# The entry of x: squares per token tile, the norm factor in a diagonal matrix, parameter loads and S5 columns moved

## The chip, the cores and the metric

The kernel runs on one core of one Trainium2 chip. Each engine (TensorE, VectorE, ScalarE, GpSimd, SyncE) works through its own queue of instructions; semaphores order them against each other. The metric is the device time of one execution in microseconds.

## The reference

One layer of a hybrid model on x of 512 tokens by 2048 (fp32). What matters here is its entry:

```python
def rms_norm(x, g):
    xf = x.astype(jnp.float32)
    y = xf * lax.rsqrt(jnp.mean(xf * xf, axis=-1, keepdims=True) + NORM_EPS)
    return (y * g.astype(jnp.float32)).astype(x.dtype)
# h = rms_norm(x, norm_mix); the columns of h @ w_in feed four mixers:
# s5_mixer, rglru_mixer, rwkv7_mixer, ssd_mixer
```

The four mixers' outputs (512 columns each) are joined and multiplied by w_out, x is added, a second norm follows, then a mixture of 64 experts of which each token uses two, and a last norm. The S5 mixer needs small tables made from its parameters (lambda, log_dt, B, C): exponentials, cosines and sines of phases, and B scaled by them.

## The kernel before

**How the work is staged.** A token tile is 128 tokens (NTT = 4 tiles), P = 128. Nearly everything lives in one large buffer `big`; the trace shows all its parts by that name. The stages are: entry of x (load, norm, turn so that the 2048 model columns lie on the partitions: `hT`, 16 k-blocks of 128 by 512 tokens), 38 projection tiles h @ w_in (L2096, each 16 k-blocks of 128x512, weights through two slabs that take turns, `ring`), with the mixers' work between the tiles, then the RWKV mixer, the output projection, routing and the experts (L2416, L2430, L2445), and the final norm (L1092 to L1094). There is no planner for the part that the change touches: the order on each engine's queue is the order of the code of its block.

**The entry, by engine.**

- SyncE (L479 to L505) issues the loads of x, one per token tile, waits for GpSimd's clearing of the parameter tables (`zero_ok`), issues the 22 loads of the tables A and B and two of mu (L491 to L494; each row of a table is 128 parameters), and then slab 0 and slab 1 of w_in (L502). From slab 2 on a slab waits for the tiles that used the slab two before it.
- ScalarE (L796 to L833) issues the loads of the S5 parameters (L797 to L804), waits for each tile of x and squares it with a running sum (L808), issues further small loads (cbc, lora, lru: L812 to L820), takes one square root for all four tiles (L822), and then the exponentials and sines for S5. After that it copies each projection tile out of PSUM (L849, `proj_out`).
- VectorE (L1102 to L1134) waits for all four sums, computes mean plus eps and its reciprocal (L1103, L1105), scales the four tiles of x in place once the root is there (L1108), copies the turned parameter tables out of PSUM (colA, colB, colC: L1111 to L1119), and multiplies the turned x by norm_mix while it copies it from PSUM into `hT` (L1132, 16 banks of 128x512). Then come the S5 phases (L1147 to L1183) and B scaled (L1216).
- TensorE (L1904 to L1921) transposes the tables A and B and the S5 columns (L1906, L1907, L1910), then x in 64 blocks of 128x128, four to a PSUM bank, with four banks taking turns (L1919), waits until all 16 banks are read (L1921), and starts the projection tiles. Behind tile 3 it turns the S5 matrices (`s5_setup`, L1929, L1935), and from tile 4 on every 11th projection matmul is followed by one S5 step (L1946, L1955).
- GpSimd (L622 to L701) clears buffers, makes the identity (`const_ok`, L640) and masks, copies the scaled B into block-diagonal form (L679), and makes the tables of cosines and sines of the 16 S5 pairs (L693 to L701), two ahead.

Of the kernel before, what the change touches and what calls it, by code (L numbers as in the profile page):

```python
# [99 lines left out]
MS, LDT, S5COL, SPA, LRDT, PHASE1, PHASE2, BBAR, SP_ = range(1, 10)  # L100
# [3 lines left out]
def build(nc, I, out):  # L104
    with ExitStack() as ctx:
# [23 lines left out]
        wk = big[:, 70:78, :]  # L129
        wglu = big[:, 78:82, :]  # L130
# [263 lines left out]
        prm_in = sem("prm_in")  # L394
# [3 lines left out]
        wglu_in, lruw_in, lora_in = sem("wglu_in"), sem("lruw_in"), sem("lora_in")  # L398
# [5 lines left out]
        h_ok = sem("h_ok")  # L404
# [68 lines left out]

        block = ctx.enter_context(nc.Block())

        @block.sync
        def _(sp):
# [3 lines left out]
            for s, (c0, wd) in enumerate(slabs):  # L481
                if s == 0:

                    sp.wait_ge(zero_ok, 1)
                    for tab, dst in ((PA, prmA), (PB, prmB)):
                        for name, (r, n) in tab.items():
                            src = I[name]
                            flat = src.rearrange(" ".join("abcd"[:len(src.shape)]) + " -> (" + " ".join("abcd"[:len(src.shape)]) + ")")
                            if name == "rw_mu":
                                flat = flat[0:3 * W]  # L490
                            sp.dma_start(dst[r:r + n, :], flat.rearrange("(r c) -> r c", c=P)).then_inc(prm_in, 16)  # L491
                    mu = I["rw_mu"]
                    sp.dma_start(prmB[MU_LORA:MU_LORA + 1, 0:LW + LA], mu[:, 3 * W:3 * W + LW + LA]).then_inc(prm_in, 16)
                    sp.dma_start(prmB[MU_LORA + 1:MU_LORA + 2, 0:LG], mu[:, 3 * W + LW + LA:]).then_inc(prm_in, 16)  # L494
# [125 lines left out]
        def _(pool):  # L620
# [5 lines left out]
            nc.gpsimd.memset(misc[:, :], 0.0)  # L626
            nc.gpsimd.memset(prmA, 0.0)
            nc.gpsimd.memset(prmB, 0.0).then_inc(zero_ok, 1)
            nc.gpsimd.memset(lruW, 0.0).then_inc(zero_ok, 1)
            nc.gpsimd.memset(epsb[:], EPS)  # L630
# [163 lines left out]
        def _(act):  # L794
            a = Steps(act, act_s)
            act.wait_ge(zero_ok, 1)  # L796
            act.dma_start(ldt[:], I["s5_log_dt"][0].rearrange("(g u) -> g u", u=2)).then_inc(ldt_in, 16)  # L797
# [7 lines left out]

            for i in range(NTT):
                act.wait_ge(x_io[i], 16)
                nc.scalar.activation(hT[:, 0:4, :].rearrange("p a n -> p (a n)"), xs[:, i, :], ACT.Square,  # L808
                                     accum_out=st[:, i:i + 1]).then_inc(ssq_ok, 1)
                act.wait_ge(ssq_ok, i + 1)  # L810
            for k, w in enumerate(("ssd_dt_bias", "ssd_a_log", "ssd_d")):
                act.dma_start(cbc[:, k, :], I[w].to_broadcast([P, SH])).then_inc(cbc_in, 16)  # L812
            act.dma_start(loraW[0:LW, 0, :], I["rw_w2"][0]).then_inc(lora_in, 16)
            act.dma_start(loraW[LW:LW + LA, 0, :], I["rw_a2"][0]).then_inc(lora_in, 16)
            act.dma_start(loraW[0:LG, 1, :], I["rw_g2"][0]).then_inc(lora_in, 16)
            act.wait_ge(zero_ok, 2)
            for r, w in enumerate(("lru_wa", "lru_wx")):
                wv = I[w][0].rearrange("(t u) i j -> u i t j", u=2)
                for u in range(2):
                    act.dma_start(lruW[64 * u:64 * u + 64, r, :, 64 * u:64 * u + 64], wv[u]).then_inc(lruw_in, 16)  # L820
            act.wait_ge(setup_ok, MS)
            nc.scalar.activation(st[:, 8:12], st[:, 4:8], ACT.Sqrt).then_inc(rs_ok, 1)  # L822
# [4 lines left out]
            nc.scalar.activation(s5v[:, 2, :], s5v[:, 1, :], ACT.Exp).then_inc(mag_ok, 1)  # L827
            act.wait_ge(setup_ok, PHASE2)
# [16 lines left out]

            def proj_out(n):
                s, c, wd, d = tiles[n]
                act.wait_ge(proj_ok, n + 1)
                nc.scalar.activation(proj[0:wd, d, :], ps[n % 2][0:wd, :], ACT.Copy).then_inc(proj_got, 1)  # L849
# [65 lines left out]
            for n in range(NT):  # L915
                if n == NT - 1:
                    take("rms_s", zroot, ACT.Sqrt, bias=epsb[:], scale=1.0 / W)
                proj_out(n)
# [177 lines left out]
        NPRM = 16 * (len(PA) + len(PB) + 2)  # L1096

        @block.vector
        def _(dve):
            v = Steps(dve, dve_s)  # L1100

            dve.wait_ge(ssq_ok, NTT)  # L1102
            v.do(nc.vector.tensor_scalar(st[:, 12:16], st[:, 0:4], 1.0 / D, EPS, ALU.mult, ALU.add))  # L1103
            v.settle()
            v.tell(nc.vector.reciprocal(st[:, 4:8], st[:, 12:16]), setup_ok, MS)  # L1105
            dve.wait_ge(rs_ok, 1)
            for i in range(NTT):
                v.tell(nc.vector.tensor_scalar(xs[:, i, :], xs[:, i, :], st[:, 8 + i:9 + i], None, ALU.mult), h_ok, i + 1)  # L1108

            dve.wait_ge(prm_tr, 1)  # L1110
            nc.vector.tensor_copy(colA[:], ps[6][:, 0:128])  # L1111
            nc.vector.tensor_copy(colB[:], ps[6][:, 128:256]).then_inc(prm_col, 1)
            dve.wait_ge(prm_col, 1)

# [3 lines left out]
            dve.wait_ge(prm_tr, 2)  # L1118
            v.tell(nc.vector.tensor_copy(colC[:], ps[7][:, 0:48]), setup_ok, S5COL)  # L1119
# [7 lines left out]

            for m in range(NTT * 4):
                i, c4 = divmod(m, 4)
                dve.wait_ge(tr_ok, m + 1)  # L1130
                g0 = PB["norm_mix"][0] + 4 * c4
                nc.vector.tensor_tensor(  # L1132
                    hT[:, 4 * c4:4 * c4 + 4, P * i:P * (i + 1)], ps[2 + m % 4][:].rearrange("p (a n) -> p a n", a=4),
                    colB[:, g0:g0 + 4].to_broadcast([P, 4, P]), ALU.mult).then_inc(tr_used, 1)  # L1134
# [768 lines left out]
        def _(pe):  # L1903
# [580 lines left out]
```

## Time and profile before

| | |
|---|---|
| median of 3 runs | 2699.86 us (2698.58 to 2702.86) |
| profiled execution, its own time | 2699.62 us |
| its span | 2697.8 us |
| TensorE matmul busy | 2366.5 us (88%) |
| VectorE, ScalarE, GpSimd busy | 760.6, 351.6, 372.2 us |
| chain that ended last | TensorE 49%, DMA 38%, VectorE 8% |

The times of the rows below are microseconds from the span's start. The chain of waits is followed back from the last instruction, at each step to what released it; "ACTq" and "SPq" are the instruction queues of ScalarE and SyncE (issues of DMAs), PEld is TensorE's weight load. An fp32 matmul that is not a transposition appears as two weight loads and two matmuls.

### The profile page before, as it was taken

Reading aid. Unit: us, or ns where it says so; the run is one execution under the profiler, and the core shown is the slowest. Engines: PE = TensorE matmul, PEld = TensorE weight load, DVE = VectorE, ACT = ScalarE, POOL = GpSimd, SP = SyncE. Lnnn points to the kernel's source line nnn. Section 1 sums busy time; section 2 is a strip of 40 time slices with the busy share of each in tenths; the row PEclk is TensorE's granted clock in tenths of the full one; section 3 lists DMA queues with packets and bytes.
Section 4 is the critical chain, followed back from the end, with each engine's and each line's share of the span. In section 5 each row is a group of like instructions: output and inputs, shape, how many; then the busy total and the mean of one; then the engine's idle time right before and its main releaser. Section 6 shows DMA issues by size and latency. Waiting matters only on the chain.

```text
span 2697.8 us, 31798 instructions
## 1 busy us (share of the span) xinstructions
PE 2366.5 (88%) x12861; PEld 1277.0 (47%) x12861; DVE 760.6 (28%) x1158; ACT 351.6 (13%) x641; POOL 372.2 (14%) x501
## 2 busy tenths in 40 slices
PE   3999999999989999869888888888888888888883
PEld 2443344455467876534444444444444444444441
DVE  4298925423553433421111000011110100111114
ACT  2100013110322222200000000000000000000001
POOL 2265500000012210011111111111011111110110
PEclk9999999999989999979999999999999999899996
DMA  5221111112022124489999999999999999999986
GB/s 147 63 78 31 63 62 52 63 63 85 4 87 72 48 72 165 175 349 428 429 429 429 426 426 418 418 421 420 413 428 415 420 415 416 419 406 410 424 376 272
DMA packets 127328, 724.00 MB, mean 268 GB/s; under 512 B 33848, under 2 KB 93052, under 8 KB 98332
## 3 DMA queue, kind: packets, MB, share of 16 engines
q1 hardware_dynamic: 100188, 704.75, 63.7%
q0 software_dynamic: 18720, 16.84, 1.8%
q10 hardware_dynamic: 8352, 1.44, 0.4%
q8 instruction: 51, 0.84, 0.1%
q14 instruction: 17, 0.14, 0.0%
HBM read 724.39 MB, written 49.81 MB: 287 GB/s over the span
## 4 chain that ended last, share of the span: by engine, by line
PE 49%; DMA 38%; DVE 8%; issue 2%; ACT 1%; ACTq 1%; SPq 1%; POOL 0%; POOLq 0%; DVEq 0%
DMA big<-in_moe_w 37%; PE ps L2096 16%; PE ps L2416 15%; PE ps L2148 5%; DVE big L1137 3%; PE ps L2314 2%; PE ps L2445 1%; PE ps L2229 1%; PE ps L2214 1%; DVE big L1267 1%; DVE big L1266 1%; PE ps L1955 1%; PE ps L1977 1%; PE ps L2335 0%; DMA big<-h_rows,gix 0%
## 5 line engine op out<-in xcount | busy, mean ns | idle before, releaser
L2416 PE MATMUL ps<-big 128*64 128x384 f32 x4096 | 715.7, 510 | 126.7 <-DMA big<-in_moe_w 126.4
L2416 PEld LDWEIGHTS ps<-big 128*64 128x64 f32 x4096 | 350.7, 143 | 503.6 <-issue 345.5
L2096 PE MATMUL ps<-big 128*128 128x512 f32 (+2 forms) x1216 | 533.1, 597 | 3.4 <-DVE big L1132 1.7
L2445 PE MATMUL ps<-big 128*64 128x512 f32 x1536 | 381.0, 650 | 51.7 <-DVE big L1870 51.7
L2096 PEld LDWEIGHTS ps<-big 128*128 128x128 f32 (+2 forms) x1216 | 227.6, 189 | 299.9 <-issue 295.8
L1867 DVE COPY big<-ps 128x384 f32<-128x384 f32 x64 | 35.7, 558 | 796.5 <-PE ps L2416 796.5
L2445 PEld LDWEIGHTS ps<-big 128*64 128x64 f32 x1536 | 113.4, 147 | 271.8 <-issue 211.2
L2148 PE MATMUL ps<-big 128*128 128x256 f32 x768 | 186.0, 391 | 12.4 <-ACT big L889 8.3
L774 POOL COPY six<-idxs 128x1 int32 (+1 forms) x64 | 11.6, 181 | 1203.1 <-DVE big L1874 1203.1
L2148 PEld LDWEIGHTS ps<-big 128*128 128x128 f32 x768 | 141.8, 191 | 38.6 <-issue 13.4
L1874 DVE COPY big<-ps 128x512 f32<-128x512 f32 x64 | 44.3, 692 | 390.4 <-PE ps L2445 390.4
L2430 PE MATMUL ps<-stacked,big 128*128 128x64 f32 x768 | 140.9, 333 | 0.0
L2430 PEld LDWEIGHTS ps<-stacked,big 128*128 128x128 f32 x768 | 138.8, 261 | 0.0
L1075 ACT ACTIVATE big<-ps 128x384 f32<-128x384 f32 x64 | 31.4, 491 | 803.7 <-PE ps L2416 803.7
L1137 DVE TENSOR_TENSOR big<-big 128x512 f32<-128x512 f32 (+8 forms) x136 | 112.3, 847 | 46.5 <-ACT big L854 41.2
L1081 ACT ACTIVATE big<-ps 128x512 f32<-128x512 f32 x64 | 38.2, 597 | 414.8 <-PE ps L2445 414.8
L849 ACT ACTIVATE big<-ps 128x512 f32<-128x512 f32 (+2 forms) x38 | 22.6, 595 | 504.2 <-PE ps L2096 504.2
L2402 PE MATMUL ps<-ident,big 128*128 128x128 f32 x520 | 71.9, 282 | 13.5 <-DMA big<-h_rows,gix 13.5
L2402 PEld LDWEIGHTS ps<-ident,big 128*128 128x128 f32 x520 | 56.4, 142 | 52.0 <-issue 52.0
L767 POOL DMA_INDIRECT big<-h_rows,gix x66 | 69.0, 1046 | 58.9 <-POOL gix L764 55.9
L777 POOL DMA_INDIRECT y_rows<-big,six x64 | 65.2, 1019 | 59.2 <-POOL six L774 55.7
L724 POOL MEMSET big<- 64x512 f32 x8 | 4.0, 517 | 453.9 <-DVE big L1557 437.5
(387 smaller groups left out, 1734.0 us busy)
## 6 DMA issues: line engine op xcount, KB each, us to landing
big<-in_moe_w SPq DMA_DIRECT2D x192, 3072.0 KB, 32.1
big<-in_w_in SPq DMA_DIRECT2D x18, 2048.0 KB, 8.6
big<-in_w_out SPq DMA_DIRECT2D x8, 1024.0 KB, 5.9
big<-y_rows SPq DMA_DIRECT2D x8, 1024.0 KB, 11.8
big<-in_x SPq DMA_DIRECT2D x4, 1024.0 KB, 8.6
big<-in_w_out SPq DMA_DIRECT2D x8, 512.0 KB, 7.0
big<-in_x SPq DMA_DIRECT2D x16, 256.0 KB, 2.7
big<-in_w_out SPq DMA_DIRECT2D x1, 4096.0 KB, 14.7
```

What stands on the lines that cost most here:

```text
L767: nc.gpsimd.indirect_dma_start(xg[k], None, hdg, bass.IndirectOffsetOnAxis(ap=gix[k][:, 0:1], axis=0), bounds_check=T * GR - 1, oob_is_err ...
L777: nc.gpsimd.indirect_dma_start(ydg, bass.IndirectOffsetOnAxis(ap=six[k][:, 0:1], axis=0), yb[k], None, bounds_check=2 * T * GR - 1, oob_is ...
L1081: nc.scalar.activation(yb[k][:, 0:512], ps[5][:], ACT.Copy).then_inc(y_ok[k], 1)
L1137: v.do(nc.vector.tensor_tensor(out, a, b, o))
L1874: nc.vector.tensor_copy(yb[k][:, 512 * q:512 * q + 512], ps[5 + q][:]).then_inc(y_ok[k], 1)
L2096: last = nc.tensor.matmul(ps[n % 2][0:wd, :], ring[s % 2][:, k, c:c + wd], hT[:, k, :], start=(k == 0), stop=(k == NC - 1))
L2148: last = nc.tensor.matmul(ps[b][:, 256 * i:256 * i + 256], ready[c][:, P * (2 * h + i):P * (2 * h + i) + P], w, start=(j == 0), stop=(j == ...
L2314: last = nc.tensor.matmul(o[:], V_[:, q, P * i:P * i + P], wo_rw[:, q, 512 * ncol:512 * ncol + 512], start=(q == 0), stop=(q == WT - 1))
L2402: last = nc.tensor.transpose(ps[h][:, P * j:P * j + P], xg[k][:, P * c:P * c + P], ident[:])
L2416: last = nc.tensor.matmul(ps[2 + w][B * g:B * g + B, 0:FF], xT[k][:, j, B * g:B * g + B], W13[k][w][:, NJ * g + j, :], start=(j == 0), sto ...
L2430: last = nc.tensor.matmul(o, uv[k][:, w, :].rearrange("p (t c) -> p c t", c=FC)[:, m], stacked[:], start=True, stop=True)
L2445: last = nc.tensor.matmul(ps[5 + q][B * g:B * g + B, :], hid[k][:, m, :], W2[k][:, m, 512 * n:512 * n + 512], start=(m == 0), stop=(m == F ...
```

## The change

Each token tile of x is squared as soon as it has landed, and its root is taken at once. VectorE puts the reciprocal of the root on the diagonal of a 128x128 matrix (`rdiag`), and x is turned by an ordinary product with this matrix in the place of the transposition; x is not scaled any more. The loads of table B (with norm_mix) and of mu go from SyncE to ScalarE's queue, ahead of the squares; those of table A go behind slab 0 on SyncE's queue; the S5 loads go behind the roots on ScalarE's queue. The turning of table A and of the S5 columns stands behind projection tile 0, VectorE's copies of them behind the banks of x, and ScalarE's copy of tile 0 ahead of its wait for the phases. The projection's first tile waits for the banks of the last token tile one by one. The rest are renamed semaphores.

```diff
--- before.py
+++ after.py
@@ -97,7 +97,7 @@
-MS, LDT, S5COL, SPA, LRDT, PHASE1, PHASE2, BBAR, SP_ = range(1, 10)
+MS, LDT, S5COL, SPA, LRDT, PHASE1, PHASE2, BBAR, SP_ = range(4, 13)
 MU_LORA = 72
@@ -127,6 +127,7 @@
         wk = big[:, 70:78, :]
+        rdiag = big[:, 76, :]
         wglu = big[:, 78:82, :]
@@ -391,17 +392,16 @@
         x_io = [sem(f"x_io{i}") for i in range(NTT)]
-        prm_in = sem("prm_in")
+        prm_in, prmB_in = sem("prm_in"), sem("prmB_in")
         s5_in = sem("s5_in")
...
         wdt_in = sem("wdt_in")
-        wglu_in, lruw_in, lora_in = sem("wglu_in"), sem("lruw_in"), sem("lora_in")
+        wglu_in, gates_in = sem("wglu_in"), sem("gates_in")
         dve_s, act_s, pool_s = sem("dve_step"), sem("act_step"), sem("pool_step")
...
         setup_ok, rs_ok = sem("setup_ok"), sem("rs_ok")
-        h_ok = sem("h_ok")
         tr_ok, tr_used = sem("tr_ok"), sem("tr_used")
@@ -471,6 +471,14 @@
+        def params(eng, tab, dst, done):
+            for name, (r, n) in tab.items():
+                src = I[name]
+                flat = src.rearrange(" ".join("abcd"[:len(src.shape)]) + " -> (" + " ".join("abcd"[:len(src.shape)]) + ")")
+                if name == "rw_mu":
+                    flat = flat[0:3 * W]
+                eng.dma_start(dst[r:r + n, :], flat.rearrange("(r c) -> r c", c=P)).then_inc(done, 16)
@@ -479,19 +487,9 @@
             for s, (c0, wd) in enumerate(slabs):
-                if s == 0:
...
+                if s == 1:
                     sp.wait_ge(zero_ok, 1)
-                    for tab, dst in ((PA, prmA), (PB, prmB)):
-                        for name, (r, n) in tab.items():
-                            src = I[name]
-                            flat = src.rearrange(" ".join("abcd"[:len(src.shape)]) + " -> (" + " ".join("abcd"[:len(src.shape)]) + ")")
-                            if name == "rw_mu":
-                                flat = flat[0:3 * W]
-                            sp.dma_start(dst[r:r + n, :], flat.rearrange("(r c) -> r c", c=P)).then_inc(prm_in, 16)
-                    mu = I["rw_mu"]
-                    sp.dma_start(prmB[MU_LORA:MU_LORA + 1, 0:LW + LA], mu[:, 3 * W:3 * W + LW + LA]).then_inc(prm_in, 16)
-                    sp.dma_start(prmB[MU_LORA + 1:MU_LORA + 2, 0:LG], mu[:, 3 * W + LW + LA:]).then_inc(prm_in, 16)
+                    params(sp, PA, prmA, prm_in)
                 if s == 5:
@@ -624,10 +622,10 @@
             nc.gpsimd.memset(misc[:, :], 0.0)
+            nc.gpsimd.memset(epsb[:], EPS)
             nc.gpsimd.memset(prmA, 0.0)
...
             nc.gpsimd.memset(lruW, 0.0).then_inc(zero_ok, 1)
-            nc.gpsimd.memset(epsb[:], EPS)
             nc.gpsimd.memset(eps64[:], 64e-5)
@@ -794,6 +792,19 @@
             act.wait_ge(zero_ok, 1)
+            params(act, PB, prmB, prmB_in)
+            mu = I["rw_mu"]
+            act.dma_start(prmB[MU_LORA:MU_LORA + 1, 0:LW + LA], mu[:, 3 * W:3 * W + LW + LA]).then_inc(prmB_in, 16)
+            act.dma_start(prmB[MU_LORA + 1:MU_LORA + 2, 0:LG], mu[:, 3 * W + LW + LA:]).then_inc(prmB_in, 16)
+            nc.scalar.activation(st[:, 40:41], epsb[:], ACT.Sqrt)
...
+            for i in range(NTT):
+                act.wait_ge(x_io[i], 16)
+                if i:
+                    act.wait_ge(ssq_ok, i)
+                nc.scalar.activation(wide(88), xs[:, i, :], ACT.Square, accum_out=st[:, i:i + 1]).then_inc(ssq_ok, 1)
+                act.wait_ge(ssq_ok, i + 1)
+                nc.scalar.activation(st[:, 4 + i:5 + i], st[:, i:i + 1], ACT.Sqrt, bias=epsb[:], scale=1.0 / D).then_inc(rs_ok, 1)
             act.dma_start(ldt[:], I["s5_log_dt"][0].rearrange("(g u) -> g u", u=2)).then_inc(ldt_in, 16)
@@ -802,29 +813,27 @@
-            for i in range(NTT):
-                act.wait_ge(x_io[i], 16)
-                nc.scalar.activation(hT[:, 0:4, :].rearrange("p a n -> p (a n)"), xs[:, i, :], ACT.Square,
-                                     accum_out=st[:, i:i + 1]).then_inc(ssq_ok, 1)
-                act.wait_ge(ssq_ok, i + 1)
             for k, w in enumerate(("ssd_dt_bias", "ssd_a_log", "ssd_d")):
                 act.dma_start(cbc[:, k, :], I[w].to_broadcast([P, SH])).then_inc(cbc_in, 16)
-            act.dma_start(loraW[0:LW, 0, :], I["rw_w2"][0]).then_inc(lora_in, 16)
-            act.dma_start(loraW[LW:LW + LA, 0, :], I["rw_a2"][0]).then_inc(lora_in, 16)
-            act.dma_start(loraW[0:LG, 1, :], I["rw_g2"][0]).then_inc(lora_in, 16)
+            act.dma_start(loraW[0:LW, 0, :], I["rw_w2"][0]).then_inc(gates_in, 16)
+            act.dma_start(loraW[LW:LW + LA, 0, :], I["rw_a2"][0]).then_inc(gates_in, 16)
+            act.dma_start(loraW[0:LG, 1, :], I["rw_g2"][0]).then_inc(gates_in, 16)
             act.wait_ge(zero_ok, 2)
...
                 for u in range(2):
-                    act.dma_start(lruW[64 * u:64 * u + 64, r, :, 64 * u:64 * u + 64], wv[u]).then_inc(lruw_in, 16)
-            act.wait_ge(setup_ok, MS)
-            nc.scalar.activation(st[:, 8:12], st[:, 4:8], ACT.Sqrt).then_inc(rs_ok, 1)
+                    act.dma_start(lruW[64 * u:64 * u + 64, r, :, 64 * u:64 * u + 64], wv[u]).then_inc(gates_in, 16)
...
+            def proj_out(n):
+                s, c, wd, d = tiles[n]
+                act.wait_ge(proj_ok, n + 1)
+                nc.scalar.activation(proj[0:wd, d, :], ps[n % 2][0:wd, :], ACT.Copy).then_inc(proj_got, 1)
...
             nc.scalar.activation(s5v[:, 2, :], s5v[:, 1, :], ACT.Exp).then_inc(mag_ok, 1)
+            proj_out(0)
             act.wait_ge(setup_ok, PHASE2)
@@ -842,11 +851,6 @@
-            def proj_out(n):
-                s, c, wd, d = tiles[n]
-                act.wait_ge(proj_ok, n + 1)
-                nc.scalar.activation(proj[0:wd, d, :], ps[n % 2][0:wd, :], ACT.Copy).then_inc(proj_got, 1)
@@ -915,7 +919,8 @@
                     take("rms_s", zroot, ACT.Sqrt, bias=epsb[:], scale=1.0 / W)
-                proj_out(n)
+                if n:
+                    proj_out(n)
                 if n == 3:
@@ -1093,45 +1098,47 @@
-        NPRM = 16 * (len(PA) + len(PB) + 2)
...
-            dve.wait_ge(ssq_ok, NTT)
-            v.do(nc.vector.tensor_scalar(st[:, 12:16], st[:, 0:4], 1.0 / D, EPS, ALU.mult, ALU.add))
-            v.settle()
-            v.tell(nc.vector.reciprocal(st[:, 4:8], st[:, 12:16]), setup_ok, MS)
-            dve.wait_ge(rs_ok, 1)
-            for i in range(NTT):
-                v.tell(nc.vector.tensor_scalar(xs[:, i, :], xs[:, i, :], st[:, 8 + i:9 + i], None, ALU.mult), h_ok, i + 1)
...
+            dve.wait_ge(const_ok, 1)
...
+            def rms_diag(i):
+                dve.wait_ge(rs_ok, i + 1)
+                v.do(nc.vector.reciprocal(st[:, 8 + i:9 + i], st[:, 4 + i:5 + i]))
+                v.settle()
+                v.tell(nc.vector.tensor_scalar(rdiag[:, P * i:P * i + P], ident[:], st[:, 8 + i:9 + i], None, ALU.mult), setup_ok, i + 1)
...
+            rms_diag(0)
             dve.wait_ge(prm_tr, 1)
-            nc.vector.tensor_copy(colA[:], ps[6][:, 0:128])
             nc.vector.tensor_copy(colB[:], ps[6][:, 128:256]).then_inc(prm_col, 1)
...
-            dve.wait_ge(ldt_in, 16)
-            v.tell(nc.vector.tensor_copy(prmC[0:16, :].rearrange("p (u n) -> p u n", u=2),
-                                         ldt[:].unsqueeze(2).to_broadcast([NPAIR, 2, S5_N])), setup_ok, LDT)
-            dve.wait_ge(prm_tr, 2)
-            v.tell(nc.vector.tensor_copy(colC[:], ps[7][:, 0:48]), setup_ok, S5COL)
-            v.settle()
-            lr, li = colC[:, 16:32], colC[:, 32:48]
...
-            ap4 = colA[:, PA["lru_a_param"][0]:PA["lru_a_param"][0] + WT]
-            v.do(nc.vector.tensor_scalar(lsp[:, 2, :], ap4, -1.0, None, ALU.mult))
-            v.settle()
-            v.tell(nc.vector.tensor_tensor(lsp[:, 0, :], ap4, lsp[:, 2, :], ALU.max), setup_ok, SPA)
...
                 i, c4 = divmod(m, 4)
+                if c4 == 2 and i + 1 < NTT:
+                    rms_diag(i + 1)
                 dve.wait_ge(tr_ok, m + 1)
...
                     colB[:, g0:g0 + 4].to_broadcast([P, 4, P]), ALU.mult).then_inc(tr_used, 1)
+            dve.wait_ge(ldt_in, 16)
+            v.tell(nc.vector.tensor_copy(prmC[0:16, :].rearrange("p (u n) -> p u n", u=2),
+                                         ldt[:].unsqueeze(2).to_broadcast([NPAIR, 2, S5_N])), setup_ok, LDT)
+            dve.wait_ge(prm_tr, 2)
+            nc.vector.tensor_copy(colA[:], ps[6][:, 0:128]).then_inc(prm_col, 1)
+            dve.wait_ge(prm_col, 2)
+            dve.wait_ge(prm_tr, 3)
+            v.tell(nc.vector.tensor_copy(colC[:], ps[7][:, 0:48]), setup_ok, S5COL)
+            v.settle()
+            lr, li = colC[:, 16:32], colC[:, 32:48]
...
+            ap4 = colA[:, PA["lru_a_param"][0]:PA["lru_a_param"][0] + WT]
+            v.do(nc.vector.tensor_scalar(lsp[:, 2, :], ap4, -1.0, None, ALU.mult))
+            v.settle()
+            v.tell(nc.vector.tensor_tensor(lsp[:, 0, :], ap4, lsp[:, 2, :], ALU.max), setup_ok, SPA)
@@ -1902,23 +1909,25 @@
             pe.wait_ge(const_ok, 1)
-            pe.wait_ge(prm_in, NPRM)
-            nc.tensor.transpose(ps[6][:, 0:128], prmA, ident[:])
+            pe.wait_ge(prmB_in, 16 * (len(PB) + 2))
             nc.tensor.transpose(ps[6][:, 128:256], prmB, ident[:]).then_inc(prm_tr, 1)
-            pe.wait_ge(setup_ok, LDT)
-            pe.wait_ge(s5_in, 16 * 8)
-            nc.tensor.transpose(ps[7][:, 0:48], prmC, ident[0:48, 0:48]).then_inc(prm_tr, 1)
             for m in range(NTT * 4):
...
                 if c4 == 0:
-                    pe.wait_ge(h_ok, i + 1)
+                    pe.wait_ge(setup_ok, i + 1)
                 if m >= 4:
...
                     c = 4 * c4 + j
-                    last = nc.tensor.transpose(ps[2 + m % 4][:, P * j:P * (j + 1)], xs[:, i, P * c:P * (c + 1)], ident[:])
+                    last = nc.tensor.matmul(ps[2 + m % 4][:, P * j:P * (j + 1)], xs[:, i, P * c:P * (c + 1)], rdiag[:, P * i:P * i + P],
+                                            start=True, stop=True)
                 last.then_inc(tr_ok, 1)
-            pe.wait_ge(tr_used, NTT * 4)
+            def s5_params():
+                pe.wait_ge(prm_in, 16 * len(PA))
+                nc.tensor.transpose(ps[6][:, 0:128], prmA, ident[:]).then_inc(prm_tr, 1)
+                pe.wait_ge(setup_ok, LDT)
+                pe.wait_ge(s5_in, 16 * 8)
+                nc.tensor.transpose(ps[7][:, 0:48], prmC, ident[0:48, 0:48]).then_inc(prm_tr, 1)
@@ -1986,7 +1995,7 @@
                 pe.wait_ge(conv_ok, WT)
-                pe.wait_ge(lruw_in, 64)
+                pe.wait_ge(gates_in, 48 + 64)
                 for q in range(WT):
@@ -2093,6 +2102,8 @@
                 for k in range(NC):
+                    if n == 0 and k % 4 == 0:
+                        pe.wait_ge(tr_used, NTT * 4 - 3 + k // 4)
                     last = nc.tensor.matmul(ps[n % 2][0:wd, :], ring[s % 2][:, k, c:c + wd], hT[:, k, :],
@@ -2101,6 +2112,8 @@
                 last.then_inc(proj_ok, 1)
+                if n == 0:
+                    s5_params()
                 if n == 3:
@@ -2152,7 +2165,7 @@
             pe.wait_ge(lot_ok, 2)
-            pe.wait_ge(lora_in, 48)
+            pe.wait_ge(gates_in, 48 + 64)
             for q in range(WT):
```

## Rows read from the trace of the kernel before

**Rows 1.** Chain of waits, 0 to 200 us: start us, us, what.

```profile
3.62 8.17 ACTq L801
...
21.30 2.01 ACT big L808 x2
...
34.97 1.28 ACT L822
...
48.52 6.08 DVE big L1132 x10
54.64 56.91 PE ps L2096 x128
...
138.44 1.89 DVE big L1137 x3
```

**Rows 2.** Timeline, 0 to 60 us: start us, us, engine, line, what [idle before].

```profile
1.58 0.44 ACTq L797 DMA_DIRECT2D ldt<-in_s_log_dt  x1
...
7.35 0.29 POOL L640 TENSOR_SCALAR_AFFINE_SELECT ident<-ident 128x128 f32<-128x128 f32 x1 [0.16 <-POOL big L638]
...
11.71 6.64 SPq L502 DMA_DIRECT2D big<-in_w_in  x2
...
36.50 4.87 DVE L1108 TENSOR_SCALAR big<-big,st 128x2048 f32<-128x2048 f32 x4 [6.68 <-ACT st L822]
41.29 0.28 DVE L1111 COPY colA<-ps 128x128 f32<-128x128 f32 x1
...
42.08 0.34 PE L1910 MATMUL ps<-ident,big 48*128 48x48 f32 x1 [23.12 <-DVE big L1116]
```

**Rows 3.** Two source lines, L479 and L804: issues, then their landing times.

```profile
L479 SPq DMA_DIRECT2D big<-in_x x4: 393/426/659, 0.8 to 2.2; - x4
...
DMA to landing us min/median/max: 4.9/8.6/12.3
...
L804 ACTq DMA_DIRECT2D big<-in_s_c_im x2: 976/1362/1748, 17.2 to 18.2; - x2
DMA to landing us min/median/max: 7.2/10.1/11.8
```

**Rows 4.** DMA issues, 0 to 60 us: KB each, median us to landing.

```profile
big<-in_w_in SPq DMA_DIRECT2D x2, 2048.0 KB, 17.3
...
big<-in_s_lambda_im ACTq DMA_DIRECT2D x1, 8.0 KB, 5.7
```

**Rows 5.** Timeline of ScalarE, 2673 to 2677 us, in the final norm.

```profile
2674.01 1.91 ACT L1092 ACTIVATE big<-big 128x2048 f32<-128x2048 f32 x1 [1.28 <-DVE big L1893]
...
2676.05 0.29 ACT L1094 ACTIVATE st<-st,epsb 128x1 f32<-128x1 f32 x1
```

**Rows 6.** Timeline of TensorE's matmuls, 560 to 565 us.

```profile
563.05 0.39 PE L2040 MATMUL ps<-maskneg,ident 128*128 128x128 f32 x2
563.27 0.39 PE L2038 MATMUL ps<-tri,sds 128*128 128x128 f32 x2
```

**Rows 7.** Stretches: length; busy us (count) of PE, PEld, DVE, ACT, POOL; clock, DMA, GB/s.

```profile
3.00:13.00 10.00, 0.00 (x0) 0.00 (x0) 0.00 (x0) 0.00 (x0) 9.30 (x22) 1.00 1.00 399
...
42.30:48.50 6.20, 6.20 (x31) 6.16 (x31) 4.69 (x9) 0.22 (x1) 0.00 (x0) 1.00 0.00 0
48.50:52.80 4.30, 4.30 (x36) 3.60 (x34) 4.29 (x8) 0.00 (x0) 0.00 (x0) 1.00 0.00 0
...
54.60:58.60 4.00, 3.96 (x6) 1.66 (x7) 3.69 (x12) 1.50 (x2) 0.00 (x0) 0.57 0.02 4
```

**Rows 8.** Timeline, 60 to 145 us.

```profile
64.25 0.84 ACT L829 ACTIVATE big<-big 128x768 f32<-128x768 f32 x1 [7.95 <-DVE big L1183]
...
70.38 0.60 ACT L849 ACTIVATE big<-ps 128x512 f32<-128x512 f32 x1 [3.03 <-PE ps L2096]
...
84.11 0.60 ACT L849 ACTIVATE big<-ps 128x512 f32<-128x512 f32 x1 [13.14 <-PE ps L2096]
...
87.14 1.26 POOL L701 TENSOR_TENSOR big<-big 128x512 f32<-128x512 f32 x1
```

More of the change, by code:

```diff
@@ L1100, in _ @@
             v = Steps(dve, dve_s)
-            dve.wait_ge(ssq_ok, NTT)
-            v.do(nc.vector.tensor_scalar(st[:, 12:16], st[:, 0:4], 1.0 / D, EPS, ALU.mult, ALU.add))
-            v.settle()
-            v.tell(nc.vector.reciprocal(st[:, 4:8], st[:, 12:16]), setup_ok, MS)
-            dve.wait_ge(rs_ok, 1)
-            for i in range(NTT):
-                v.tell(nc.vector.tensor_scalar(xs[:, i, :], xs[:, i, :], st[:, 8 + i:9 + i], None, ALU.mult), h_ok, i + 1)
+            dve.wait_ge(const_ok, 1)
[5 more added lines that the diff above has]
+            rms_diag(0)
             dve.wait_ge(prm_tr, 1)
-            nc.vector.tensor_copy(colA[:], ps[6][:, 0:128])
             nc.vector.tensor_copy(colB[:], ps[6][:, 128:256]).then_inc(prm_col, 1)
             dve.wait_ge(prm_col, 1)
+            for m in range(NTT * 4):
+                i, c4 = divmod(m, 4)
+                if c4 == 2 and i + 1 < NTT:
+                    rms_diag(i + 1)
+                dve.wait_ge(tr_ok, m + 1)
+                g0 = PB["norm_mix"][0] + 4 * c4
+                nc.vector.tensor_tensor(
+                    hT[:, 4 * c4:4 * c4 + 4, P * i:P * (i + 1)], ps[2 + m % 4][:].rearrange("p (a n) -> p a n", a=4),
+                    colB[:, g0:g0 + 4].to_broadcast([P, 4, P]), ALU.mult).then_inc(tr_used, 1)
             dve.wait_ge(ldt_in, 16)
@@ L1126, in _ @@
             v.tell(nc.vector.tensor_tensor(lsp[:, 0, :], ap4, lsp[:, 2, :], ALU.max), setup_ok, SPA)
[L1128 to L1134, printed above, removed]
             def op(out, a, b, o):
```

## The prediction

> **What bounds the kernel now.** I read the chain of waits first, because the change touches only the first 55 us and the question is which engine holds the start there. Up to 54.64 us no projection runs. The chain lies on ScalarE's queue: the issue of one small load alone takes 8.17 us, the first square waits behind it until 21.3, the square root comes at 34.97 (a table load, then the root) and the first projection starts at 54.64 [rows 1]. The timeline adds what lies between the last two: VectorE scales x for 4.9 us, and TensorE turns it from 42.3 on, after 23 us of idleness [rows 2]. ScalarE had no reason in x for being so late: the four x loads are issued from 0.8 us on, the first is there 4.9 us after its issue, the last 12.3 us after its own [rows 3]. From 54.64 on the chain is TensorE's projection tiles, and from about 138.4 on VectorE's S5 pairs [rows 1], which TensorE's steps between the tiles feed. Nothing in these rows is tied to an absolute time, so what the start gains or loses should reach the end one to one.
>
> I measure the change at one landmark: the end of projection tile 1, where ScalarE begins to copy it at 84.11 us [rows 8]. By then the moved S5 columns have been paid as well.
>
> **ScalarE's new order.** It issues 6 DMAs (4 of table B, 2 of mu) from 1.6 us on, such an issue takes 0.44 us [rows 2], so they are out at about 4.3. Table load 1.28 [rows 1], one small Sqrt 0.29 [rows 5]: 5.9. Tile 0 of x has landed at 0.8 + 4.9 = 5.7. In the final norm Square and Sqrt of one tile take from 2674.01 to 2676.05 plus 0.29 = 2.33 us, and no table load stands between the roots and squares there [rows 5], so the alternation costs none here. Root of tile 0: about 8.3. Tile 3 lands at 2.2 + 12.3 = 14.5 [rows 3]; its root is there at 16.9. This replaces the common root after 34.97 + 1.28. The S5 issues that stalled ScalarE now come behind the roots.
>
> **VectorE.** Out: the two small operations on the sums and the four scalings of x, 4.87 us on the path [rows 2]. In: per tile one reciprocal and one 128x128 product with a column scalar. The trace has no such product; a 128x128 copy out of PSUM takes 0.28 [rows 2]. With the small reciprocal and two hand-overs, 0.4 to 0.8; I take 0.55. Diagonal 0 is there at 8.9, the last at 17.5.
>
> **Table B.** Its last issue is at about 4.3. A like small load on ScalarE's queue under the same x traffic landed 5.7 us after its issue [rows 4]: 10.0. The lower bound is no delay at all, 4.3 (the start would then wait for diagonal 0, 8.9), the upper one the landing of x itself, 14.5. I take 10.0. One transposition more: 10.5. The identity, complete at 7.6 [rows 2], is no limit. So TensorE starts to turn x at 10.5 rather than 42.3.
>
> **The turning product.** This is the part that gets dearer. Now it is 64 transpositions of one pass; afterwards 64 ordinary fp32 products with 128 columns, of two weight loads and two matmuls each. The trace has just these in another stage: the two instructions of one line there take 0.22 us (563.05 to 563.27) [rows 6], so 0.223 us a block at full clock, 0.446 at half. Before, the transpositions ran 31 in 6.2 us and then 36 in 4.3 us [rows 7]. The clock column gives 1.00 for both; it is the rate that tells that TensorE came out of its idleness at the lower of its two levels (1.2 GHz) and rose to 2.4 GHz at 48.5. I take the same 6.2 us for the new start: 13.9 blocks at 0.446, then 50.1 at 0.223 = 11.2 us, together 17.4. VectorE's drains, 6.08 us for 10 banks [rows 1], so 2.4 for four, plus the diagonal make 3.0 us a token tile against TensorE's 16 x 0.223 = 3.6, so TensorE paces it; tile 3's diagonal comes long before its turn at 24. The first projection starts at 10.5 + 17.4 = 27.9. It needn't wait for the last banks, since k-blocks 0 to 3 need bank 13 only.
>
> The Trainium skill, page Perfetto Trace Analysis, section Transposes, says that a logical transposition should be a transpose and not a standard matmul. The trace agrees on the price: 0.223 a block instead of 0.12 at full clock. By this rule alone the change would lose 64 x 0.103 = 6.6 us; what the rule leaves out is that the product lets the scalings and the wait for all four tiles go.
>
> **Slab 0 of w_in.** Now issued at 11.71 behind the parameters [rows 2], afterwards at about 2.9 directly behind x. Before, the two slabs landed 17.3 us after their issue in the middle, together with the S5 loads [rows 4]. Afterwards x is through at about 13, and at 399 GB/s [rows 7] 2.1 MB more take 5.3: it lands at about 20. The upper bound is the old landing, 11.7 + 17.3 = 29.0, one us behind 27.9. I take no cost.
>
> **Tiles 0 and 1, and the S5 columns between them.** Tile 0 took 70.38 - 54.64 = 15.74 us [rows 1, 8]. In its first four us the granted clock was 0.57 in the mean, so half of full for most of them [rows 7], right after transpositions paced by VectorE; that cost 4.0 x 0.43 = 1.7. With TensorE now in ordinary products without a gap I let the clock hold: 14.0. Then come the two transpositions, 0.34 us for the small one [rows 2] and about as much for the other, 0.6 in all. Tile 1: 13.7 (70.38 to 84.11). Landmark: 27.9 + 14.0 + 0.6 + 13.7 = 56.2 against 84.1, 27.9 us earlier.
>
> **What the moved steps wait for.** The two transpositions behind tile 0 wait for the S5 loads, and tile 1, next in TensorE's queue, with them. These loads are now issued from 17 us on. Before, the last of them, c_im, was issued at 18.2 and took up to 11.8 to land: 30.0, some 17 us after x was through [rows 3]. Afterwards 17 + 12 to 17 + 17, so 29 to 34, while tile 0 ends at 41.9. The slack of 8 us is the cover; without it each microsecond of lateness is one at the end. Table A rides behind slab 0 on SP's queue, slab 1 behind it; it is needed at 56.
>
> The Trainium skill, page DMA: Bandwidth & Descriptors, section Queues, rings and completion order, says that each DMA engine goes round robin between the queues, a packet at a time. This fits the 8.17 us issue: ScalarE's small packets advance one by one beside x's. By it the S5 loads get through faster beside slab 1's short rows than beside x, the lower end of 29 to 34.
>
> VectorE copies the S5 columns (colC) at about 42.4, as before, so relative to the projections 28 us later. What hangs on them took 64.25 - 54.6 = 9.7 us to the phases (the sines begin there), and 24.2 more to GpSimd's second table, complete at 88.4 [rows 8]. Afterwards: 52.1 and 76.3. TensorE's S5 set-up stands behind tile 3, at 56.2 + 2 x 13.7 = 83.6, and GpSimd's block copies that it needs come before the tables. No cost, slack over 7 us. ScalarE's copy of tile 0 now stands before its wait for the phases, so tile 2 isn't held.
>
> **Sum.** 2699.62 (the profiled execution's own time; span 2697.8 and 1.8 around it) - 27.9 = 2671.7. That execution lies 0.24 below the median of the three runs, 2699.86; I forecast 2672.
>
> **Rivals.**
> 1. *TensorE stays at the lower clock through the turning* (chance 0.12). For it: the rows of this form cover only some products in a stage that was fast before. Against it: even transpositions saw the clock rise after 6.2 us [rows 7]. Turning 64 x 0.446 = 28.5, projection from 39.0, tile 0 again 1.7 dearer: 12.8 us less gained, 2684.6.
> 2. *The start hangs on a load* (0.10): table B or x's tile 3 comes later, or slab 0 at 31 rather than 20, because an issue is held up by a full queue as the 8.17 us one was [rows 1]. 3 to 6 us less gained: 2675 to 2678.
> 3. *The S5 loads hold tile 1 back* (slower; 0.03). The place is TensorE's wait behind tile 0. It costs one to one what they come after 41.9, and turns the whole into a loss from 41.9 + 27.9 = 69.8 on; at 80 us it would be 2710. For it: the longest issue of the whole start is one of these. Against it: before, they were through at 30.0 though begun beside x.
> 4. *The gain is taken back later* (0.02, no change, 2700): the S5 pairs or the expert stage turn out paced by something that does not start earlier. No row of the chain shows such a thing.
>
> **From this to the numbers.** Forecast 0.73, at 2672. Its own spread: TensorE's start at 8.9 and half the time at the lower clock give 2669; table B at 14 and a lower clock once more in tile 0 give 2677.5; stretches of lower clock in later stages may come or go, some 2 us either way. The range 2667 to 2682 takes in rival 2 and leaves out rivals 1, 3 and 4. A difference of 0.2%, 5.4 us, is what a measurement here can tell from none. Faster by more: 0.73 + 0.12 + 0.10 = 0.95; within: 0.02; slower: 0.03.
>
> **What would show it.** ScalarE: four pairs of square and root between 6 and 17 us, no table load among them. TensorE: first product at 10 to 11, 128 matmuls over 17 to 18 us with the rate doubling inside them, first projection at 27 to 29, at full clock from its first matmul, slab 0 landed before. Between tiles 0 and 1 less than 1 us without a projection. The VectorE piece at 138.44 comes at about 110.5, and each later stage 28 us earlier. The forecast is wrong if a block keeps taking 0.43 us, if TensorE waits for a load at about 42, or if that VectorE piece comes less than 25 us earlier.

## The result and the profile after

The changed kernel takes 2672.59 us (median of 4 runs, 2669.5 to 2673.07) against 2701.36 before: ratio 0.9893, 95% interval 0.988 to 0.9906. Forecast 2672. Run again beside its variants (r1_change) it gave 2671.77 against 2700.11, ratio 0.9903 (0.9886 to 0.9919). The profiled execution took 2669.5, the lowest of the four, with a span of 2667.7. The intervals of both ratios lie below 1, so the gain of about 1% is clear of the scatter.

The chain of waits of the changed kernel, 0 to 200 us (start us, us, what):

```profile
2.09 0.67 ACTq L480
...
4.25 5.83 DMA big<-in_rw_mu
10.66 16.65 PE ps L1922 x128
27.31 13.73 PE ps L2107 x32
41.34 41.41 PE ps L2107 x96
...
109.64 1.89 DVE big L1144 x3
```

Of ScalarE's queue only the short issues of table B's loads are left in it, until 4.25; the stalled issues of the S5 loads are gone. The last load of table B (the second one of mu) holds TensorE until 10.1, then the chain is TensorE's to 82.8. VectorE's piece that stood at 138.44 [rows 1] stands at 109.64, 28.8 earlier.

One long issue is left at the start, in another queue. SyncE's first small load behind slab 0 took 9.68 us to issue, and 10.78 in e4_s5_first; the same load directly behind x, with no slab ahead of it, took 0.41 before and 0.52 in e1_order.

```profile
3.63 9.68 SPq L480 DMA_DIRECT2D big<-in_s_d  x1
```

Here nothing waits for it, since table A is first used at 40.9. Why such an issue takes so long, no run shows; that the queue was full, as rival 2 of the prediction has it, is a guess.

The timeline of the changed kernel (start us, us, engine, line, what, [idle before <- releaser]) answers to rows 2 and 5:

```profile
4.59 1.28 ACT L799 ACT_TABLE_LOAD   x1 [4.59 <-issue]
5.89 0.20 ACT L799 ACTIVATE st<-epsb 128x1 f32<-128x1 f32 x1
6.13 1.91 ACT L805 ACTIVATE big<-big 128x2048 f32<-128x2048 f32 x1
...
8.56 0.17 DVE L1110 RECIPROCAL st<-st 128x1 f32<-128x1 f32 x1 [8.56 <-ACT st L807]
8.76 0.36 DVE L1112 TENSOR_SCALAR big<-ident,st 128x128 f32<-128x128 f32 x1
...
10.21 0.45 PE L1913 MATMUL ps<-ident,big 128*128 128x128 f32 x1 [10.21 <-DMA big<-in_rw_mu]
...
13.75 1.91 ACT L805 ACTIVATE big<-big 128x2048 f32<-128x2048 f32 x1 [0.17 <-DMA big<-in_x]
...
15.79 0.29 ACT L807 ACTIVATE st<-st,epsb 128x1 f32<-128x1 f32 x1
...
27.15 13.90 PE L2107 MATMUL ps<-big 128*128 128x512 f32 x32
...
55.31 0.60 ACT L830 ACTIVATE big<-ps 128x512 f32<-128x512 f32 x1 [0.42 <-PE ps L2107]
```

The last row is the landmark, the copy of tile 1: 55.31 instead of 84.11 [rows 8], 28.8 earlier, forecast 27.9. The stretches of the changed kernel (columns as in rows 7) show the rate of the product and the clock of tile 0:

```profile
10.40:15.70 5.30, 5.30 (x27) 5.30 (x27) 2.03 (x5) 5.07 (x8) 4.41 (x14) 1.00 1.04 376
15.70:27.10 11.40, 11.40 (x104) 11.40 (x104) 9.47 (x17) 0.35 (x2) 2.61 (x4) 1.00 1.14 282
27.10:31.10 4.00, 4.00 (x12) 1.85 (x12) 0.85 (x3) 0.00 (x0) 0.00 (x0) 1.00 0.95 181
```

27 matmuls in 5.3 us are 0.196 each, 104 in 11.4 are 0.110: half speed first, then full, as the transpositions had it before [rows 7]. The two stretches together count 131 for the 128, since table B's transposition falls into the first and what spans a border is counted on both sides. The column of the granted clock gives 1.00 for both, as it did for the transpositions; the lower level is read off the rate alone. Tile 0 runs at 1.00, without the 0.57 of before.

### The profile page after: what moved, and what is told of

It is laid out like the page before. It is cut to its first block, busy times and chain, and to the rows that moved or that the text cites. A ratio compares the mean times of both kernels' runs of the same rounds, so it can differ in the third digit from the quotient of the medians.

```text
span 2667.7 us, 31933 instructions
## 1 busy us (share of the span) xinstructions
PE 2368.4 (89%) x12925; PEld 1283.9 (48%) x12925; DVE 758.4 (28%) x1160; ACT 351.7 (13%) x644; POOL 372.7 (14%) x501
## 4 chain that ended last, share of the span: by engine, by line
PE 50%; DMA 38%; DVE 8%; issue 2%; ACT 1%; SPq 1%; POOL 0%; ACTq 0%; POOLq 0%; DVEq 0%
DMA big<-in_moe_w 37%; PE ps L2107 17%; PE ps L2429 15%; PE ps L2161 5%; DVE big L1144 3%; PE ps L2327 2%; PE ps L2458 1%; PE ps L2242 1%; PE ps L2227 1%; DVE big L1274 1%; DVE big L1273 1%; PE ps L1922 1%; PE ps L1964 1%; PE ps L1986 1%; PE ps L2348 0%
## 5 line engine op out<-in xcount | busy, mean ns | idle before, releaser
L2429 PE MATMUL ps<-big 128*64 128x384 f32 x4096 | 729.5, 518 | 127.2 <-DMA big<-in_moe_w 126.7
L2458 PE MATMUL ps<-big 128*64 128x512 f32 x1536 | 365.7, 628 | 51.8 <-DVE big L1877 51.8
```

What stands on the lines that cost most here:

```text
L2429: last = nc.tensor.matmul(ps[2 + w][B * g:B * g + B, 0:FF], xT[k][:, j, B * g:B * g + B], W13[k][w][:, NJ * g + j, :], start=(j == 0), sto ...
L2458: last = nc.tensor.matmul(ps[5 + q][B * g:B * g + B, :], hid[k][:, m, :], W2[k][:, m, 512 * n:512 * n + 512], start=(m == 0), stop=(m == F ...
```

## The experiments

"Landmark" is the start of ScalarE's copy of projection tile 1 in the profiled execution; "rest" is that execution's span less its landmark.

| run | landmark | first projection | span | rest | time (median) |
|---|---|---|---|---|---|
| before | 84.11 | 54.64 | 2697.8 | 2613.7 | 2700 to 2701 |
| changed | 55.31 | 27.15 | 2667.7 | 2612.4 | 2672.59 |
| e1_order | 72.78 | 45.01 | 2689.7 | 2616.9 | 2691.93 |
| e2_order_columns | 61.40 | 33.24 | 2675.2 | 2613.8 | 2680.81 |
| e3_scale_turn | 54.07 | 24.88 | 2672.5 | 2618.4 | 2671.26 |
| e4_s5_first | 73.55 | 45.39 | 2691.9 | 2618.4 | 2692.14 |
| e5_tableB_sync | 59.98 | 31.81 | 2677.7 | 2617.7 | 2679.43, one run |
| e6_all_banks | 56.15 | 27.91 | 2672.3 | 2616.2 | 2674.05, one run |
| e7_columns_first | 76.28 | 48.50 | 2696.1 | 2619.8 | 2697.92, one run |
| e8_warm | 52.93 | 24.77 | 2667.9 | 2615.0 | 2669.69, one run |
| r1_change | 54.44 | 26.27 | 2670.7 | 2616.3 | 2671.77 |
| r2_scale_turn | 54.09 | 25.09 | 2672.8 | 2618.7 | 2671.30 |
| r3_warm | 52.99 | 24.82 | 2667.0 | 2614.0 | 2669.81 |
| r4_warm_tableB_late | 52.15 | 23.98 | 2665.4 | 2613.3 | 2669.99 |

The code blocks below are the edits, shortened; lines with # say in words where they stand.

In all fourteen profiles the last projection copy comes 632.9 to 634.8 us behind the landmark; the scatter arises behind it. The rest scatters from 2612.4 to 2619.8; the changed kernel alone gives 2612.4 and 2616.3. So the landmark tells a microsecond or less, the time 3 to 7 us from one execution to the next. Before has only one profile, and 11 of the 13 others have a longer rest than its 2613.7: whether the later stages give back a microsecond or two of the gain stays open. In every run but the changed kernel's first the median gains less in time than the profile gains at the landmark (e1_order 8.2 and 11.3, e2_order_columns 19.3 and 22.7).

**e1_order**

```diff
 # ScalarE, in the kernel before
+ squares of the four tiles; wait MS; one Sqrt
  S5 loads (ldt, lambda, b, c)
- squares of the four tiles
  cbc, lora, lru loads
- wait MS; one Sqrt
```

> The kernel before, with one change on ScalarE's queue: squares and the common root stand ahead of the S5 loads; scaling, transposition and the S5 columns ahead of x stay. Theory (the columns hold TensorE as soon as ScalarE doesn't): root at about 17.5, x scaled by 23, but TensorE waits for the S5 loads, now issued from 18 us on, until 33 to 35; first projection at about 46.5 instead of 54.6, so 8 us less, ratio 0.997. Rival (the late root was the whole cost): the turning starts at about 20 and the first projection at about 33, 21 us less, ratio 0.992.

Ratio to before 0.9965 (0.9953 to 0.9978), 8.2 us less; landmark 11.3 earlier. The root comes at 17.2 instead of 36.3, but TensorE's rows show who holds it now:

```profile
17.52 0.45 PE L1906 MATMUL ps<-ident,big 128*128 128x128 f32 x1 [17.52 <-DMA big<-in_rw_mu]
17.76 0.42 PE L1907 MATMUL ps<-ident,big 128*128 128x128 f32 x1
32.88 0.31 PE L1910 MATMUL ps<-ident,big 48*128 48x48 f32 x1 [14.70 <-DMA big<-in_s_c_im]
```

The S5 loads, now behind the squares, keep it until 32.9. The theory holds, the rival's 33 is excluded. The 3 us more at the landmark than expected are 1.5 in the first projection (45.0) and 1.7 of the lower clock, which tile 0 did not have here (in the columns of rows 7, where before has 0.57 at this place):

```profile
45.00:49.00 4.00, 3.99 (x10) 1.84 (x11) 3.69 (x12) 1.50 (x2) 0.00 (x0) 1.00 0.01 4
```

**e2_order_columns**

```diff
 # e1_order, and
 # TensorE
- transpose(prmC) ahead of x
+ if n == 0: wait LDT; wait s5_in; transpose(prmC)   # behind projection tile 0
 # VectorE: the copies LDT and colC with SPA go behind the 16 banks
 # ScalarE: proj_out(0) ahead of its wait for PHASE2
```

> As e1_order, and the turning of the S5 columns with VectorE's copies of them moved behind projection tile 0; one root for all tiles, scaling and transposition stay. Theory: tile 0 scaled at 19.3, turning from about 19.5, first projection at 32.5, the lower clock again in tile 0; copy of tile 1 at about 62 instead of 84.1, 22 us less, ratio 0.992. Order alone then carries three quarters of the gain of 28.8. Rival (the product with the diagonal is what carries it): less than 12 us.

Ratio 0.993 (0.9913 to 0.9946), 19.3 us less; landmark 22.7 earlier, 22 expected. Two moves, the order on ScalarE's queue and the S5 columns behind tile 0, carry 22.7 of the 28.8, with one common root, scaling and transposition as before. The agreement with 22 is in part luck: the first projection came at 33.2 and not 32.5, and 1.7 of the 22.7 is the lower clock in tile 0, which was expected and did not come. At the first projection they carry 21.4 of 27.5.

**e3_scale_turn and r2_scale_turn**

```diff
 # the changed kernel
- tensor_scalar(rdiag[:, P*i:P*i+P], ident[:], st[:, 8+i:9+i], None, mult)
+ tensor_scalar(xs[:, i, :], xs[:, i, :], st[:, 8+i:9+i], None, mult)
- matmul(ps[2+m%4][...], xs[:, i, P*c:P*c+P], rdiag[:, P*i:P*i+P])
+ transpose(ps[2+m%4][...], xs[:, i, P*c:P*c+P], ident[:])
```

> The changed kernel, with the product undone: VectorE scales each token tile in place (four times 1.28 us) and TensorE transposes it; all orders and the root per tile stay. Theory: VectorE becomes the pace, 16 x 0.69 + 4 x 1.5 us, first projection at about 27.5 as with the product, tile 0 then 1.7 us dearer by the lower clock: copy of tile 1 at about 57.5 against 55.3, 2 us more than the changed kernel. Rival (the product is worth the scaling that it saves): first projection at 31 or later, 4 us or more. Other rival (the product is dearer than it is worth, 64 x 0.1 us): 3 to 6 us faster than the changed kernel.

> Scaling in place and transposition again, beside the product on the same chip. Theory (the landmark carries to the end): 1.2 us less than the changed kernel, 2670 to 2672. Rival (the lower clock that transpositions bring costs later): 1 to 3 us more than the changed kernel.

Ratio to before 0.9887 (0.987 to 0.9903) and 0.9894 (0.9878 to 0.9911); beside the product on the same chip 2671.30 against 2671.77, no difference that can be told. At the landmark it is 1.2 and 0.4 us earlier than the product, where e3's theory had it 2 later. The first projection came at 24.9 and not 27.5, for three reasons. VectorE drains a bank in 0.61 and not 0.69 when the banks stand ready, 1.3 us over 16. Tile 0 was scaled at 8.59, before table B was there, so that only three scalings lie on the path. And the first projection started 1.1 us before the last bank was drained. Against them the first drain began at 11.5, a microsecond later than assumed. VectorE's and TensorE's rows of e3_scale_turn:

```profile
8.59 1.29 DVE L1112 TENSOR_SCALAR big<-big,st 128x2048 f32<-128x2048 f32 x1
...
13.10 1.41 DVE L1112 TENSOR_SCALAR big<-big,st 128x2048 f32<-128x2048 f32 x1
14.44 2.46 DVE L1124 TENSOR_TENSOR big<-ps,colB 128x512 f32<-128x512 f32 x4
```

```profile
18.35 1.97 PE L1922 MATMUL ps<-ident,big 128*128 128x128 f32 x16 [1.81 <-DVE big L1112]
22.41 2.68 PE L1922 MATMUL ps<-ident,big 128*128 128x128 f32 x16 [2.10 <-DVE big L1112]
24.88 14.92 PE L2106 MATMUL ps<-big 128*128 128x512 f32 x32
```

TensorE turns a token tile in 2.0 us instead of 3.6 and waits for VectorE; VectorE needs 3.8 with the scaling. The two ways are worth the same within a microsecond: what the product spares VectorE it costs TensorE. Up to the first projection the transposition is 2.3 us ahead (1.2 beside r1_change); tile 0 then takes 14.8 us (14.6) instead of 13.7 at the lower clock, which stands here from 23.5 to 26.9:

```profile
23.50:26.90 3.40, 3.40 (x12) 2.37 (x10) 2.58 (x6) 0.00 (x0) 0.00 (x0) 0.50 1.17 326
```

**e4_s5_first**

```diff
 # the changed kernel, ScalarE
+ S5 loads ahead of the squares, behind table B
```

> The changed kernel, with the S5 loads issued ahead of the squares on ScalarE's queue again. Theory (the queue's stalled issues were the cost): issues until about 23, root of tile 0 at 25.6, turning from 26.2, first projection at about 43.5: 16 us of the gain of 28.8 go. Rival (loads interfere little, tiles of x are awaited anyway): under 3 us.

Ratio to before 0.9965 (0.9951 to 0.9979). The landmark is 18.2 us later than the changed kernel's, 16 expected. The issues end at 24.2 and the first root comes at 27.7; the loads cost ScalarE the time of its queue, nothing else: TensorE starts to turn at 28.6, 18.2 later, and from there to the landmark it takes 44.9 us in both kernels. The root is 2 us later than expected, and so is the landmark. Neither of the two moves is worth more than some 11 us without the other: the order alone gives 11.3 (e1_order), all the rest without the order 10.6 (this run), all the rest without the columns 7.8 (e7_columns_first).

```profile
13.51 7.98 ACTq L806 DMA_DIRECT2D big<-in_s_c_re  x2
21.52 2.70 ACTq L806 DMA_DIRECT2D big<-in_s_c_im  x2
24.25 1.28 ACT L807 ACT_TABLE_LOAD   x1 [24.25 <-issue]
```

**e5_tableB_sync**

```diff
- ScalarE: params(act, PB, prmB, prmB_in); 2 loads of mu
+ SyncE, behind x and ahead of slab 0: wait zero_ok; params(sp, PB, prmB, prmB_in); 2 loads of mu
```

> The changed kernel, with the loads of table B and mu on SyncE's queue behind x and ahead of slab 0. Theory (a load behind x in the same queue lands with x): table B turned at 14 to 16 instead of 10.2, first projection at 31 to 33 instead of 27.15, copy of tile 1 at 59 to 61 instead of 55.3. Rival (table B is hidden by the tiles of x): no change, 55.3.

Landmark 59.98, 4.7 us later; table B is turned at 14.54 instead of 10.21. In the queue of x, behind its 4 MB, these small loads come 4.3 us later than on ScalarE's queue (one run).

**e6_all_banks**

```diff
- if n == 0 and k % 4 == 0: wait(tr_used, 13 + k // 4)
+ if n == 0 and k == 0:     wait(tr_used, 16)
```

> The changed kernel, the first projection waits for all 16 banks at once as before the change. Theory: first projection at 28.2 instead of 27.15, copy of tile 1 at 56.3. Rival (a gap in TensorE's work brings the lower clock in tile 0 back): another 1.7 us, 58.

Landmark 56.15: 0.8 later than in the first profile of the change, no more than two executions of one kernel differ by (r1_change). TensorE's wait for VectorE in it is 0.87 us, so that much is the edit's; tile 0 ran at full clock (1.00), so this gap did not bring the lower clock in this one run.

**e7_columns_first**

```diff
 # the changed kernel
+ TensorE: wait LDT; wait s5_in; transpose(prmC) ahead of the product, not behind tile 0
+ VectorE: LDT and colC ahead of the 16 banks (the diagonals get a semaphore of their own)
```

> The changed kernel, the S5 columns turned and copied ahead of x again (their loads stay behind the roots). Theory (then TensorE waits for the last S5 load): turning of x from about 32, first projection at about 49, copy of tile 1 at about 77 instead of 55.3. Rival (the loads are quick when x is through): turning from about 22, copy of tile 1 at about 67.

Landmark 76.28, 21.0 later; the theory holds. TensorE's row tells when the last S5 load is there, the wait that the change hides behind tile 0:

```profile
31.92 0.31 PE L1918 MATMUL ps<-ident,big 48*128 48x48 f32 x1 [21.56 <-DMA big<-in_s_c_im]
```

From this row to the first projection it takes 16.6 us with the product, and 12.1 in e1_order with x scaled beforehand and transposed. Where everything waits for the same load, the way with the product is 4.5 us dearer.

**e8_warm and r3_warm**

```diff
 # the changed kernel, TensorE
+ wait zero_ok
+ for i in range(20): matmul(ps[7][:, 0:P], ones[:], ones[:])
```

> The changed kernel, and TensorE, which idles until 10.2 us, multiplies a matrix of ones by itself 20 times from about 1.6 us on (work that nobody reads). Theory (the slow first third of the turning is the clock after idleness): the turning runs at 0.223 us a block from its first one on, 14.3 us in all, first projection at about 24.8 instead of 27.15, copy of tile 1 at 52.9 instead of 55.3. Rival (the first blocks are slow for another reason, such as the wait for VectorE): no change.

> The changed kernel with 20 unused products of ones ahead. Theory: 2.4 us less than the changed kernel, ratio to it 0.9991. Rival (the later stages swallow it): no difference.

Landmark 52.93 and 52.99 (52.9 expected): 2.4 us before the first profile of the change, 1.5 before r1_change, whose own slow part was shorter. Stretches of e8_warm: the unused work takes over the slow part, and the product runs at full speed from its first block.

```profile
1.60:5.40 3.80, 3.76 (x18) 3.76 (x19) 0.00 (x0) 0.82 (x1) 3.76 (x7) 1.00 0.94 302
5.40:8.20 2.80, 2.72 (x25) 2.53 (x23) 0.00 (x0) 2.76 (x5) 2.64 (x7) 1.00 1.03 426
10.20:24.80 14.60, 14.60 (x130) 14.53 (x131) 11.86 (x22) 5.44 (x9) 7.20 (x17) 1.00 1.07 309
```

18 matmuls in 3.8 us, 25 in 2.8, then 130 in 14.6. So the slow part belongs to whatever TensorE does first after idleness, not to the product or to waits for VectorE. That it is the clock is inferred from the rate, which is half; the column gives 1.00. The time, 2669.81 (ratio to before 0.9893, 0.9877 to 0.991) against r1's 2671.77, points the same way but is within the scatter.

**r4_warm_tableB_late**

```diff
 # r3_warm, TensorE
- wait prmB_in; transpose(prmB) ahead of x
+ if m == 1: wait prmB_in; transpose(prmB)   # behind the second bank of x
```

> As r3_warm, and TensorE turns table B behind the second bank of x instead of ahead of the first, so that the product starts with diagonal 0 at about 9.0 and not with table B at 10.2. Theory: first projection at 23.6, copy of tile 1 at 51.8 (changed kernel 55.3, e8_warm 52.9), 3.5 us less than the changed kernel. Rival (VectorE, which gets norm_mix later, becomes the pace): first projection at 24.5 to 25, no gain over r3_warm.

Landmark 52.15, 0.8 us before r3_warm; 1.1 were expected. The product starts at 8.93, but VectorE gets norm_mix at 11.4 and TensorE waits for VectorE once, 0.31 us at 13.16, for the diagonal of tile 1. It has the earliest landmark of all, 2.3 before r1; its time, 2669.99 (ratio to before 0.9894, 0.9877 to 0.991), can't be told from the changed kernel's.

**r1_change**

> The changed kernel unaltered, beside its variants on one chip. Copy of tile 1 at 55.3 as in its first profile; its time 2672 to 2673, the first profile of 2669.5 having been a low one: the stages from 690 us on scatter by some 3 us from execution to execution.

Landmark 54.44 and not 55.31. Table B was there 0.15 us earlier, and the rate of the product doubled earlier in this execution, so that the turning took 16.0 and not 16.7 us. Two executions of one kernel differ by 0.9 us here, 0.7 of it through this rate. The time, 2671.77, came just under the 2672 to 2673 expected; one of its four executions took 2677.75.

## Why the prediction was right, point by point

- *ScalarE's queue holds the start.* Shown: e4_s5_first gives back 18.2 us of 28.8 by that one order. The order by itself gains only 11.3 (e1_order), since TensorE then waits for the same loads.
- *The S5 columns behind tile 0 cost nothing and their loads land between 29 and 34.* Shown: 31.9 to 32.9 where TensorE waited for them (e7_columns_first, e1_order). In the changed kernel TensorE reaches them at 40.9 without a wait and loses some 0.4 us (0.6 forecast). Their issues did stall again, 7.02 us for c_re from 20.23 on, but no longer ahead of anything. Taken back, the move costs 21.0.
- *Table B at 10.0, start of the turning at 10.5.* Measured 10.2 and 10.45. On SyncE's queue 14.5 (e5_tableB_sync).
- *x's tile 3 at 14.5, last root at 16.9.* It landed about 13.7 (ScalarE waited 0.17 us for it), root at 16.1, never on the path.
- *The last diagonal at 17.5, long before its turn at 24.* This step was wrong, at no cost. VectorE makes a diagonal between two banks of the tile before, so the last was complete at 23.1, and TensorE came to tile 3 at about 23.6 (27.15 less 32 matmuls of 0.11). The slack was 0.5 us and not 6; with the faster start it is gone, and TensorE waits 0.17 us for a diagonal in r3_warm, 0.31 in r4_warm_tableB_late.
- *The product: 17.4 us, of it 6.2 at half speed.* Measured 16.7 (10.45 to 27.15), of it 5.3 at half speed, and 3.7 in r1_change. The block at full clock took 0.22 as worked out. That the slow part comes of the idleness before it is shown by e8_warm; that it is the clock rests on the halved rate.
- *Slab 0 at about 20.* Its landing was 17.0 after the issue at 2.95: 20.0.
- *Tile 0 at full clock.* Held in all nine profiles with the product. The reason that I gave, transpositions bring the lower clock back in tile 0, is only half right: before, e3_scale_turn and r2_scale_turn have it, e1_order and e2_order_columns don't. Before and e1_order did the same just ahead of tile 0, 12 transpositions in 3.4 us with TensorE busy for 1.7, and had 0.57 and 1.00 behind it. It was worth 1.7 us of the sum, and these 1.7 us can't be put down to the product: in part they are luck.
- *Table A.* The prediction names no time at which it is needed; TensorE turns it ahead of the S5 columns, at 40.88, and found it there.
- *Later stages follow one to one.* The last projection copy moved from 718.8 to 690.0, by 28.8 like the landmark; from there on it is shown only within the scatter. First to last gather of the experts took 1467.8 us before, 1467.3 and 1472.4 in two executions of the changed kernel.

That 2672.59 lies within 0.6 us of the forecast is partly luck, at a scatter of 3 us and more. The test is the landmark, 55.31 and 54.44 against 56.2: the difference is the turning, 16.7 and 16.0 us against 17.4, most of it by its shorter slow part, and 0.2 to 0.3 from the other terms.

One argument was wrong in its weight, not in the sum. I set the price of the product (6.6 us) against the scaling and the wait for all four tiles. The wait goes by the root per tile, not by the product: e3_scale_turn keeps the transposition and loses nothing. The root per tile, table B's earlier loads and the wait bank by bank together put its first projection 8.4 us ahead of e2_order_columns'; table B's queue is worth 4.7 of the changed kernel (e5_tableB_sync), the root per tile was not tried alone.

The Trainium skill, page Perfetto Trace Analysis, section Transposes, says that a logical transposition should be a transpose and not a standard matmul. These runs agree: a token tile takes TensorE 3.6 us as products and 2.0 as transpositions, and departing from the rule bought nothing, 0.4 to 1.2 us dearer at the landmark and no difference in the time.

What stays open: why an issue stalls for 7 to 11 us, why the lower clock sometimes follows transpositions and sometimes not, and which of the later stages' stretches at the lower clock come from where they fall; no run changed these alone.

## What to carry to other kernels

Look at what an engine's queue issues ahead of its first useful instruction: small loads there can hold the whole start, and here moving them paid in full (28.8 us and not 11) only together with moving the work that waits for them on another engine. Let a row of the same form, however far away in the trace, price a new operation; 0.223 us a block from a row pair at 563 us gave the turning to within 1 us. For a change at the start, a landmark just behind it separates variants to within a microsecond where the whole time scatters by 3 to 7.

## What was not expected of the hardware

TensorE at the start ran at half rate for 3.7 us (r1_change), 5.3 (the first profile of the change) and 6.2 (before) of steady work, and twenty unused products of a constant matrix took this time off the useful ones: 1.5 to 2.4 us at the landmark. VectorE drains a 128x512 bank at 0.60 to 0.61 us apiece when banks stand ready, and at one per 0.89 when it waits for each (TensorE's four blocks), though the single instruction shows 0.67 to 0.69 in both.
